# A three-block transformer kernel: TensorE transposes the identity in 18 places where it waits

## The reference

```python
x = first_block(x, mem, ...)    # differential attention, dense SwiGLU, HGRN2, 8 routed experts, final norm
x = second_block(x, ...)        # retention + latent attention, then block attention, with layer norms
return third_block(x, c_3, ...) # mLSTM, convolution and sparse attention branches, merged
```

```python
y = xf * lax.rsqrt(jnp.mean(xf * xf, axis=-1, keepdims=True) + EPS)
```

## Time and profile before

| what | value |
|---|---|
| median of 3 runs | 3275.2 us (3274.37 to 3276.45) |
| the profiled execution | 3276.38 us, of which the span is 3274.6 us |
| mean granted TensorE clock | 0.955 |
| PE matmul busy | 3025.7 us, 92% |
| PE weight load busy | 2622.7 us, 80% |
| DVE busy | 2017.8 us, 62% |
| ACT busy | 1524.6 us, 47% |
| DMA | 606 MB, 185 GB/s on average |

### The profile page before, as it was taken

How to read it: one execution, slowest core, us unless ns; L and a number is a source line. 1 busy time by engine, 2 the same in 40 slices (tenths; PEclk the granted TensorE clock), 3 DMA queues, 4 the chain that set the end, 5 groups by cost and what they waited for, 6 DMA issues and landing times. The chain is left out here.

```text
span 3274.6 us, 41596 instructions
## 1 busy us (share of the span) xinstructions
PE 3025.7 (92%) x17205; PEld 2622.7 (80%) x17205; DVE 2017.8 (62%) x2251; ACT 1524.6 (47%) x1723; POOL 24.0 (1%) x41
## 2 busy tenths in 40 slices
PE   6989988789999999989999998999889897998898
PEld 6879886678888889678888887898688697985797
DVE  4547646445445457488898987455455645777755
ACT  4443343334334346367777775433334444432453
POOL 0001000000000000000000000000000000000000
PEclk9989998789999999999999999999899898998999
DMA  5338641044445456479999997442344152345142
GB/s 184 127 103 269 221 146 49 9 180 180 180 172 189 180 189 249 180 296 350 372 344 352 369 350 284 164 158 59 122 155 155 65 178 80 129 133 180 53 150 101
DMA packets 207350, 606.02 MB, mean 185 GB/s; under 512 B 19936, under 2 KB 78121, under 8 KB 163898
## 3 DMA queue, kind: packets, MB, share of 16 engines
q1 hardware_dynamic: 201282, 587.97, 49.5%
q0 software_dynamic: 3872, 12.71, 1.3%
q10 hardware_dynamic: 2008, 2.67, 0.3%
HBM read 602.26 MB, written 1.05 MB: 184 GB/s over the span
## 5 line engine op out<-in xcount | busy, mean ns | idle before, releaser
L1934 DVE TENSOR_TENSOR w_lo<-ring,w_hi 128x2048 fp32r<-128x2048 f32 x336 | 769.5, 2292 | 350.9 <-ACT w_hi L1836 346.9
L1836 ACT ACTIVATE w_hi<-ring 128x2048 fp32r<-128x2048 f32 x336 | 643.1, 1915 | 373.0 <-PE ps L1785 193.3
L344 DVE TENSOR_TENSOR w_lo<-ring,w_hi 128x2048 fp32r<-128x2048 f32 (+2 forms) x228 | 472.2, 2073 | 519.2 <-ACT w_hi L335 518.7
L335 ACT ACTIVATE w_hi<-ring 128x2048 fp32r<-128x2048 f32 (+2 forms) x228 | 396.5, 1740 | 698.0 <-PE ps L448 538.9
L448 PE MATMUL ps<-h_hi,w_hi 128*128 128x256 f32 x1608 | 463.2, 288 | 26.6 <-DVE w_lo L344 19.1
L448 PE MATMUL ps<-h_lo,w_hi 128*128 128x256 f32 x1608 | 459.1, 285 | 0.0
L448 PE MATMUL ps<-h_hi,w_lo 128*128 128x256 f32 x1608 | 458.8, 285 | 0.0
L448 PEld LDWEIGHTS ps<-h_hi,w_hi 128*128 128x128 f32 x1608 | 312.8, 195 | 30.9 <-issue 26.4
L448 PEld LDWEIGHTS ps<-h_lo,w_hi 128*128 128x128 f32 x1608 | 312.7, 194 | 0.3
L448 PEld LDWEIGHTS ps<-h_hi,w_lo 128*128 128x128 f32 x1608 | 312.7, 194 | 0.0
L1761 PE MATMUL ps<-w_hi,h_hi 128*128 128x512 f32 x448 | 178.9, 399 | 4.9 <-DVE w_lo L1934 4.9
(11 more groups left out here) (531 smaller groups left out, 5993.5 us busy)
## 6 DMA issues: line engine op xcount, KB each, us to landing
ring<-in_moe_w_gate_up SPq DMA_DIRECT2D x224, 1024.0 KB, 6.8
ring<-in_moe_w_down SPq DMA_DIRECT2D x112, 1024.0 KB, 6.6
ring<-in_w_in SPq DMA_DIRECT2D x54, 1024.0 KB, 6.7
ring<-in_w_in_even SPq DMA_DIRECT2D x28, 1024.0 KB, 6.6
ring<-in_dense_w_gate_up SPq DMA_DIRECT2D x22, 1024.0 KB, 7.9
ring<-in_w_in_odd SPq DMA_DIRECT2D x16, 1024.0 KB, 6.8
arena<-in_w_ada POOLq DMA_DIRECT2D x24, 512.0 KB, 4.8
ring<-in_w_out_even SPq DMA_DIRECT2D x12, 1024.0 KB, 7.3
```

The lines of the kernel that those rows point to most:

```text
L335: k.nc.scalar.activation(self.part(k.w_hi, b, m), src, ACT.Copy).then_inc(k.hi_ready, 1)
L344: k.nc.vector.tensor_tensor(self.part(k.w_lo, b, m), src, self.part(k.w_hi, b, m).bitcast(F32), ALU.subtract).then_inc(k.lo_ready, 1)
L1836: nc.scalar.activation(high(g, h), raw(g, h), ACT.Copy).then_inc(k.hi_ready, 1)
L1934: nc.vector.tensor_tensor(low(g, h), raw(g, h), high(g, h).bitcast(F32), ALU.subtract).then_inc(k.lo_ready, 1)
```

## The change

A helper issues `n` transposes of the 128x128 identity `k.ident` (float32) into a PSUM bank. It has no wait, and no instruction waits for it except through the order of PE's own queue. It is called in 18 places with 652 transposes in all; some of the places are neighbours, at both sides of a meeting of the stages, and the 18 lie in 14 waits of PE. Where the bank was in use for squares, the squares are put into other banks; in the routed experts this adds a wait of ACT for its own first square sum.

```diff
-    def stage(self, name, side=None, extra=(), source=(), features=None, norm=False):
+    def stage(self, name, side=None, extra=(), source=(), features=None, norm=False, first_turns=0, last_turns=0):
...
             def _(pe):
                 beside = steps.get("pe")
+                turn_identity(k, first_turns, 7)
                 for step in (beside or {}).get(0, ()):
                     step()
...
+                used = [self.place(r, 0, r.count - 1).bank for r in runs[-2:]] + [self.place(runs[-1], 0, 0).bank]
+                turn_identity(k, last_turns, 6 if norm is False else 2 * next(b for b in range(SLOTS) if b not in used))
...
+def turn_identity(k, n, bank):
+
+    for _ in range(n):
+        k.nc.tensor.transpose(k.ps[:, bank, 0:P], k.ident[:, :], k.ident[:, :])
...
-                squares(half, x, lambda t: k.ps[:, 2 * half + t, :])
+                squares(half, x, lambda t: k.ps[:, t, :])
...
+            turn_identity(k, 22, 7)
             pe.wait_ge(chosen_ready, 1)
...
+            turn_identity(k, 28, 7)
             pick(0)
+            turn_identity(k, 40, 7)
             for e in range(EXPERTS):
...
             give_back(EXPERTS - 1)
+            turn_identity(k, 72, 3)
...
                 act.wait_ge(x_complete, t + 1)
-                nc.scalar.activation(k.ps[:, 2 * t:2 * t + 2, :].rearrange("p b n -> p (b n)"), x[:, t, :], ACT.Square,
+                if t:
+                    act.wait_ge(squares_summed, t)
+                nc.scalar.activation(k.ps[:, 0:2, :].rearrange("p b n -> p (b n)"), x[:, t, :], ACT.Square,
                                      accum_out=k.stat[:, t:t + 1]).then_inc(squares_summed, 1)
...
-    attention(k, "latent_attention", groups, v.work)
-    s.stage("out_even", source=v.cat_parts,
+    attention(k, "latent_attention", groups, v.work, last_turns=8)
+    s.stage("out_even", source=v.cat_parts, first_turns=26, last_turns=72,
```

More of the change, by code:

```diff
@@ L1104, in unit, with attention @@
     return u
-def attention(k, name, groups, work):
+def attention(k, name, groups, work, last_turns=0):
     nc = k.nc
@@ L1170, in _ @@
                     last.then_inc(values_done, 1)
+            turn_identity(k, last_turns, 7)
         @st.block.vector
@@ L1431, in _ @@
             over_experts(pe, expert)
+            turn_identity(k, 58, 3)
         @st.block.scalar
@@ L2343, in _ @@
             last.then_inc(transposed, 1)
+            turn_identity(k, 30, 7)
         @st.block.vector
@@ L2499, in block1 @@
     head_norm(k, "subln", v.cat[:, 0:6, :], column(k, "a_subln"), v.tmp)
-    s.stage("out_a", source=[v.cat_parts], side=lambda st: residual_scales(k, st), norm=True)
+    s.stage("out_a", source=[v.cat_parts], side=lambda st: residual_scales(k, st), norm=True, last_turns=36)
     swiglu(k, "dense", k.x, k.h, v.dense_hidden, v.dense_gated, v.dense_raw,
@@ L2509, in block1 @@
     head_norm(k, "out_norm_b", v.cat[:, 0:6, :], column(k, "b_out_norm"), v.tmp_b, gate=v.g)
-    s.stage("out_b", source=[v.cat_parts], side=lambda st: residual_scales(k, st), norm=True,
+    s.stage("out_b", source=[v.cat_parts], side=lambda st: residual_scales(k, st), norm=True, last_turns=34,
             extra=[(v.gain_row, w["moe_norm"].partition_broadcast(P))])
@@ L2923, in block2 @@
         groups.append(([u], r, MOBA_DH, v.cat2[r:r + 64, h // 2, :], v.g2[r:r + 64, h // 2, :]))
-    attention(k, "block_attention", groups, v.work2)
-    s.stage("out_odd", source=[v.cat2_parts], extra=extra,
+    attention(k, "block_attention", groups, v.work2, last_turns=8)
+    s.stage("out_odd", source=[v.cat2_parts], extra=extra, first_turns=26, last_turns=96,
             side=lambda st: layer_then_rms_scales(k, st, (0, 1), w["ln_g_2"][1], w["ln_b_2"][1]))
@@ L3550, in block3 @@
     attention(k, "sparse_attention", groups, v.work)
-    s.stage("merge_gates", side=lambda st: gates_steps(k, st, v))
-    s.stage("branches", side=lambda st: merge_steps(k, st, v), source=v.branches,
+    s.stage("merge_gates", side=lambda st: gates_steps(k, st, v), last_turns=32)
+    s.stage("branches", first_turns=20, last_turns=24, side=lambda st: merge_steps(k, st, v), source=v.branches,
             extra=[(k.rows[:, 0, :], w["norm_post_3"].flatten().partition_broadcast(P))])
-    s.stage("out_merged", side=lambda st: gated_end(k, st, v, out), source=[v.merged_parts])
+    s.stage("out_merged", first_turns=20, side=lambda st: gated_end(k, st, v, out), source=[v.merged_parts])
 AREA = 21250
```

## The result

The changed kernel takes 3254.38 us (median of 6 runs, 3250.45 to 3255.25) against 3275.82 us for the kernel before in the same session (6 runs, 3274.37 to 3282.89). The ratio is 0.9926, with a 95% interval of 0.9915 to 0.9938: 21 us or 0.7% faster. The profiled execution is the fastest of the six, 3250.45 us.

What follows compares the result with a forecast made beforehand. PE was taken as the bound, busy 92% of the span, with 295 us at the lower clock. Terms 22.0 - 1.5 + 2.2 + 0.6 - 1.2 = 22.1 us took the profiled 3276.4 to 3254.3, median 3253 us; range 3245 to 3266.

Steps and rivals of the forecast that it cites:

- HGRN2: 30 transposes starting at half clock end 0.8 us late; 7.67 us of half clock behind run full; net +2.2 us.
- the router: Behind `out_b` (34 transposes): 1.6 us forecast, from the 4.1 us stretch only.
- Routed experts: 22 start at half clock, 1.4 us too long; `pick(0)` gains 2.0; net +0.6, between -3 and +2.6; 40 counted separately.
- `in_even`: Stage behind a fill of 72: 1.8 us gained and not 2.3, as DVE needs 3.32 us for eight `h_lo`.
- Transposes hold the clock: In the filled waits: identity transposes count as work, about 0.11 us each at full clock, against the Trainium skill's rule.
- Fills end before the meeting: At stage ends fills just fit the waits; at attention ends the 8 are 0.43 us late, twice, costing 0.9.
- (b): Clock held, but half the gain lost again to DVE's split of the next half panel or a load; 3264 us; chance 0.17.
- (a): Identity transposes do not hold the clock, so it falls inside fills and they end late; 3309 us; chance 0.09.
- (c): Fills and lateness cancel: clock falls in small holes before and after fills; 3271 to 3279 us; chance 0.05.
- (d): More than forecast: neighbouring dips, after the router and in attention stages, go too; 3243 us; chance 0.05.

Runs made afterwards that it cites:

- the twin: Changed kernel with all transposes left out, the squares' new banks and ACT's added wait kept: 3274.78 us, ratio 1.0001 to the kernel before; its profiled execution spans 3272.4 us.
- the six ends alone: Changed kernel with transposes only at the six ends of stages with a norm (36, 58, 34, 72, 72, 96): 3265.61 us, ratio 0.9969 to the kernel before.
- the fitted counts: Changed kernel with late groups cut (22 removed, 28 to 17, 30 to 26, four other fills cut): 3249.95 us, ratio 0.9923 to the kernel before.
- nine more: Transposes only at the six stage ends with a norm, nine more in each (45, 67, 43, 81, 81, 105): 3274.41 us, ratio 0.9995 to the kernel before.
- half counts: Transposes only at the six stage ends with a norm, half of each number (18, 29, 17, 36, 36, 48): 3274.68 us, ratio 0.9999 to the kernel before.
- with 8 columns: Changed kernel with each pair of transposes made one fp32 identity matmul on 8 columns, 652 instructions as before: 3299.31 us, ratio 1.0081 to the kernel before.
- twenty more fills: Fitted version (late groups cut) with some 20 more waits filled, 1080 transposes instead of 603: 3220.67 us, ratio 0.9832 to the kernel before.

## Why the prediction was right, and where it was off

**The size.** Forecast 3253, measured 3254.4. The sum was 22.1 us for one execution against another; the twin above gives 23.7, and the two medians 21.4. The terms were less good than their sum: HGRN2 and the router brought 3.6 us more than forecast, the others 2.0 less. That these errors cancel is luck. The gain of each stage in us, worked out from the starts of PE behind each meeting in the timelines of the change and of the twin:

| stage | forecast | measured |
|---|---|---|
| behind `out_a` (36) | 1.6 | 1.5 |
| behind the dense experts (58) | 2.2 | 1.6 |
| HGRN2 (30), with the stage behind it | 2.2 | 4.4 |
| router, behind `out_b` (34) | 1.6 | 3.0 |
| routed experts (22, 28, 40) | 0.6 + 1.6 | 1.9 |
| `in_even` (72) | 1.8 | 0.6 |
| attention end and `out_even` (8, 26) | 2.0 | 2.2 |
| `in_odd` (72) | 1.8 | 1.7 |
| attention end and `out_odd` (8, 26) | 2.4 | 2.0 |
| behind `out_odd` (96) | 1.0 | 1.8 |
| `branches` with the stage ahead of it (32, 20) | 2.1 | 1.7 |
| last stage (24, 20) | 1.3 | 1.4 |
| stages without a fill | 0 | -0.2 |

**Transposes hold the clock: right.** In the change's trace all long fills have 0.109 us for each transpose and a clock of 1.00 to the end, the 96 too. That PE comes to them at full clock is not certain, as I had it: in the traces of the six ends alone and of the fitted counts, the clock is low when the 72 of the experts' end begin; they take 8.56 and 8.74 us and end 0.3 and 0.5 us after DVE. The Trainium skill's rule ("TensorE: Matmul & The Clock Gate", Part 4), by which the full clock does not engage for transposes, is not borne out by this case (the durations on the page are of bf16 transposes, these are fp32). What behaves as the rule says is something else: matmuls with 8 columns (48 of them at 0.50 for 10.3 us).

**Fills end before the meeting: right.** DVE's end in `out_a`, at 209.26, is 0.37 us ahead of PE's start at 209.63, as before, so nothing was delayed. In the latent attention PE is last, as forecast (timeline of the change, DVE and then PE):

```profile
2319.25 0.42 DVE L1240 TENSOR_TENSOR arena<-ps,arena 128x256 f32<-128x256 f32 x1 [0.42 <-PE ps L1175]
...
2319.05 1.04 PE L562 MATMUL ps<-ident 128*128 128x128 f32 x8
2320.50 3.03 PE L562 MATMUL ps<-ident 128*128 128x128 f32 x26 [0.41 <-PEq L171]
```

DVE ends at 2319.67, PE at 2320.09: 0.42 late for the forecast 0.43. In block attention it is 0.56.

**HGRN2: the mechanism right, the term too small.** The stretch of the 30 has a clock of 0.84 (505.00:509.10 above), that is 4.1 x 2 x 0.16 = 1.3 us at half clock, so PE was 0.4 us late at the meeting and not 0.8; against the twin the stage lost 0.8. The next stage's third group of scores comes 516.77 - 509.49 = 7.28 us after its first, before it was 527.02 - 516.62 = 10.40: 3.1 gained, forecast 3.0. The other 2.1 us come from a later dip of the clock, which is shorter in the change. The rest of the stage, in the kernel before and then in the change:

```profile
545.00:585.20 40.20, 31.44 (x174) 23.28 (x172) 36.11 (x42) 7.73 (x11) 0.00 (x0) 0.94 0.00 1
```

```profile
534.80:572.80 38.00, 29.27 (x173) 21.46 (x171) 35.55 (x41) 7.74 (x11) 0.00 (x0) 0.98 0.00 1
```

It is 40.2 us at 0.94 and then 38.0 at 0.98. I had counted only the first dip. Whether the fill takes the later one away is open: this stage takes 68.7 us in the kernel before, in the twin and with nine more, but 66.4 in two runs that have no fill here either (the six ends, and their half counts), and 63.1 to 63.5 in the four runs with the fill of transposes.

**The router: a term that was missing.** I gave `out_b`'s fill the stretch of 4.1 us and no more, and took the 48 products of the earlier trace rows as at half clock in any case. In the change they begin at full clock and lose it on the way, which is 1.5 us more. This one repeats: the stage takes 18.2 to 19.0 us in the four traces without the 34 or with half of them, and 15.0 to 16.4 in the five with them.

**Routed experts: the row was misread.** I had the 22 end 1.4 us late and the experts' start gain 0.6. They began at half clock and stayed there to the last, 4.7 us up to the sums in a wait of 3.3, and another 0.58 of it had passed before they started: some 2 us late. From the meeting to the first product it is 23.7 us against 23.5. The net is -0.2, within my range of -3 to +2.6.

**`in_even`: the gain was given back in this execution.** The fill of 72 worked. PE comes to its next wait 2.1 us sooner than in the kernel before, and 1.3 sooner than in the twin. That wait is not filled (timelines of PE, the kernel before and then the change, and behind each its stretch):

```profile
2067.32 0.36 PE L448 MATMUL ps<-h_hi,w_hi 128*128 128x256 f32 x1 [4.01 <-DVE w_lo L344]
...
2067.30:2074.30 7.00, 6.98 (x46) 7.00 (x47) 2.08 (x1) 1.74 (x3) 0.00 (x0) 0.76 0.48 178
```

```profile
2046.53 0.55 PE L448 MATMUL ps<-h_hi,w_hi 128*128 128x256 f32 x1 [4.01 <-DVE w_lo L344]
...
2046.50:2053.50 7.00, 6.97 (x36) 7.00 (x37) 2.09 (x1) 1.75 (x3) 0.00 (x0) 0.57 0.47 177
```

The wait is 4.01 us in both. Behind it the clock is 0.76 before and 0.57 in the change, so PE gets 36 instructions done in 7 us instead of 46. It is not the fill that does this to the next wait. Here is the same stretch in the run with only the six ends, which has the same 72:

```profile
2059.90:2066.90 7.00, 7.00 (x46) 7.00 (x47) 2.05 (x1) 1.72 (x3) 0.00 (x0) 0.76 0.47 178
```

It has 0.76 again; every trace but the change's has 0.76 to 0.78. With the six ends alone the stage takes 169.2 us from meeting to meeting, for 171.3 in the change and 171.9 in the twin. So rival (b) didn't come true here; one execution had bad luck.
The stages that the change doesn't touch show the same: against the twin two gain 1.3 and 1.4, one 1.5, one loses 1.7, and two in a row lose 2.5. With the small ones they cancel to -0.2.

**The rivals.** (a) needs work that doesn't hold the clock, and with such work it happens. (b) and (c) would have left 11 us or less; 21 came. A time like that of (c), 0.9999, came only with half the counts, where the holes are 2 to 5 us long. (d) was in part true (the router, HGRN2 perhaps).

## What to carry to other kernels

Where PE waits for some microseconds and dense work follows, the clock that it loses costs about half the length of the slow stretch behind the wait. Filling the wait with fp32 transposes of 128 columns into a bank that nobody reads gave that back; matmuls with 8 columns did not. Fill to within a few tenths of a microsecond of the end of the wait and no further: half a fill brought nothing, and nine transposes too many took back the gain. Where the clock is already low and the wait is short, a fill can end late and bring nothing (the 22).

One profiled execution carries some microseconds of luck with the clock. Compare stage by stage with an execution that agrees up to the first edit, look whether a stage's gain comes back in other runs that have the same fill, and take sizes from the medians.

## What was not expected of the hardware

The clock's dips differ between executions of the same instructions. The first instruction of the fill behind `out_a`'s products, ahead of which nothing differs between these kernels, starts at 205.05 in the change, 207.66 with 8 columns, 212.89 with the six ends alone and 212.94 with the fitted counts. The stretch from 121 to 183 us in the change and then in the six ends alone:

```profile
121.00:183.00 62.00, 51.45 (x284) 40.89 (x282) 33.83 (x104) 32.99 (x100) 0.00 (x0) 0.88 0.10 32
...
121.00:183.00 62.00, 53.37 (x270) 42.16 (x271) 30.54 (x100) 30.00 (x98) 0.00 (x0) 0.83 0.13 42
```

The same short waits cost more clock in one execution than in another; what decides it no run here shows. So a wait that looks harmless in one trace may cost in the next, and it fits that twenty more fills brought more than one trace had let me expect.
